# The four transposes of an expert's chunk: in one row ahead of the next chunk's up product, or one at a time between its steps

## What is computed

```python
def swiglu(t, wg, wu, wd):
    return (jax.nn.silu(t @ wg) * (t @ wu)) @ wd

def moe_ffn(h, router_w, wg, wu, wd):
    ...
    for e in range(N_EXPERTS):
        y = y + gates[:, e:e + 1] * swiglu(t, wg[e], wu[e], wd[e]).astype(jnp.float32)
```

## Time and profile before

| what | value |
|---|---|
| median of 3 runs | 1448.1 us (1447.97 to 1448.22) |
| the profiled execution | 1447.98 us |
| its span in the trace | 1446.2 us |
| PE busy | 1427.1 us (99%), 7084 matmuls |
| PE loads busy | 1189.5 us (82%) |
| DVE busy | 1194.8 us (83%) |
| ACT busy | 1034.2 us (72%) |
| granted TensorE clock, mean | 0.999 of 2.4 GHz |
| DMA | 454.11 MB, 314 GB/s over the span |

### The profile page before, as it was taken

One profiled execution on the slowest core, in us unless ns is written; L12 is line 12 of the kernel. 1 busy time (PEld: TensorE's weight loads), 2 busy tenths in 40 slices (PEclk: granted clock), 3 DMA queues, 4 the chain that ended last, 5 costly groups with the idle time before them and its releaser, 6 DMA issues.

```text
span 1446.2 us, 20820 instructions
## 1 busy us (share of the span) xinstructions
PE 1427.1 (99%) x7084; PEld 1189.5 (82%) x7084; DVE 1194.8 (83%) x1381; ACT 1034.2 (72%) x1280; POOL 18.6 (1%) x15
## 2 busy tenths in 40 slices
PE   9999999999999999999999999999999999999997
PEld 7988888887987788888888888888888888888885
DVE  7777565556877798899889999989889989889997
ACT  6766444455576677887787787787778778777775
POOL 0000000000000200000000000000000000001001
PEclk9999999999999999999999999999999999999999
DMA  9435965544524499999999999999999999999991
GB/s 374 176 130 210 372 236 204 201 174 175 183 110 160 164 422 402 355 403 382 364 394 389 380 368 398 381 363 392 384 351 397 390 378 370 393 375 373 420 394 71
DMA packets 68899, 454.11 MB, mean 314 GB/s; under 512 B 9456, under 2 KB 9712, under 8 KB 17008
## 3 DMA queue, kind: packets, MB, share of 16 engines
q1 hardware_dynamic: 61056, 432.47, 76.9%
q10 hardware_dynamic: 6640, 16.78, 3.3%
q0 software_dynamic: 1152, 4.19, 0.7%
HBM read 438.21 MB, written 15.20 MB: 314 GB/s over the span
## 4 chain that ended last, share of the span: by engine, by line
PE 94%; DVE 2%; ACT 2%; issue 1%; DMA 0%; DVEq 0%; SPq 0%; ACTq 0%
PE psum L493 26%; PE psum L495 26%; PE psum L494 26%; PE psum L845 7%; PE psum L848 3%; PE psum L907 2%; ACT lru_b L1025 1%; PE psum L500 1%; PE psum L664 0%; PE psum L605 0%; PE psum L520 0%; DVE xs L1442 0%; PE psum L890 0%; DMA gain<-gains 0%; ACT w_hi L1012 0%
## 5 line engine op out<-in xcount | busy, mean ns | idle before, releaser
L1330 DVE TENSOR_TENSOR w_lo<-ring,w_hi 128x1024 fp32r<-128x1024 f32 x812 | 941.0, 1219 | 51.9 <-ACT w_hi L1012 51.1
L1012 ACT ACTIVATE w_hi<-ring 128x1024 fp32r<-128x1024 f32 x812 | 807.4, 1053 | 55.2 <-PE psum L495 49.9
L493 PE MATMUL psum<-w_hi,hT_both 128*128 128x512 f32 (+1 forms) x1120 | 434.3, 388 | 1.3 <-DVE hT_both L1341 1.3
L495 PE MATMUL psum<-w_hi,hT_both 128*128 128x512 f32 (+1 forms) x1120 | 426.7, 381 | 0.0
L494 PE MATMUL psum<-w_lo,hT_both 128*128 128x512 f32 (+1 forms) x1120 | 425.9, 380 | 0.0
L493 PEld LDWEIGHTS psum<-w_hi,hT_both 128*128 128x128 f32 x1120 | 210.7, 188 | 42.7 <-DVE hT_both L1341 3.7
L495 PEld LDWEIGHTS psum<-w_hi,hT_both 128*128 128x128 f32 x1120 | 210.6, 188 | 41.2
L494 PEld LDWEIGHTS psum<-w_lo,hT_both 128*128 128x128 f32 x1120 | 211.0, 188 | 38.4 <-issue 0.4
L493 PE MATMUL psum<-w_hi,act_hi 128*128 128x512 f32 x560 | 218.7, 391 | 0.0
L495 PE MATMUL psum<-w_hi,act_lo 128*128 128x512 f32 x560 | 218.2, 390 | 0.0
L494 PE MATMUL psum<-w_lo,act_hi 128*128 128x512 f32 x560 | 218.2, 390 | 0.0
(11 more groups left out here) (243 smaller groups left out, 885.8 us busy)
## 6 DMA issues: line engine op xcount, KB each, us to landing
ring<-moe_gate SPq DMA_DIRECT2D x112, 1024.0 KB, 7.1
ring<-moe_up SPq DMA_DIRECT2D x112, 1024.0 KB, 7.5
ring<-moe_down SPq DMA_DIRECT2D x112, 1024.0 KB, 7.2
ring<-in_units SPq DMA_DIRECT2D x19, 1024.0 KB, 7.9
ring<-dense_gate SPq DMA_DIRECT2D x14, 1024.0 KB, 4.8
ring<-dense_up SPq DMA_DIRECT2D x14, 1024.0 KB, 4.8
ring<-dense_down SPq DMA_DIRECT2D x14, 1024.0 KB, 4.8
ring<-out_units SPq DMA_DIRECT2D x8, 1024.0 KB, 8.1
```

Of the source, the lines that this page charges most:

```text
L493: pe.matmul(dst, s_hi, m_hi, start=start, stop=False)
L495: return pe.matmul(dst, s_lo, m_hi, start=False, stop=stop)
L1012: act.activation(w_hi[:, h % AHEAD, :], ring[:, n % RING, (h % 2) * HCOLS:(h % 2 + 1) * HCOLS], ACT.Copy).then_inc(hi_ready, 1)
L1330: dve.tensor_tensor(w_lo[:, h % AHEAD, :], ring[:, (h // 2) % RING, (h % 2) * HCOLS:(h % 2 + 1) * HCOLS], w_hi[:, h % AHEAD, :].bitcast(F3 ...
```

## The change

On PE the function `turn_prod` is replaced by `turn_piece(c, f)`, which makes one of the four transposes: the wait for `prod_ready` is at the first piece, the increment of `prod_tr` at the last. For chunks 0 to 5 the pieces now stand inside the unit (up, c, 0) of the next chunk, one ahead of each of its four products. So three 512-column matmuls lie between one transpose and the next, where none did. The transposes of the seventh chunk stay in a row where they were. On ACT and DVE `turned_hi(c - 1)` and `turned_lo(c - 1)` move from ahead of the splits of (gate, c, 1) to ahead of the second split of (up, c, 0), that is behind three more splits. The number of instructions of each kind is the same.

```diff
             def expert_item(item, final):
-                def turn_prod(c):
-
-                    pe.wait_ge(prod_ready, item * ENC + (NCH + c + 1))
-                    for f in range(ETC):
-                        mm = pe.transpose(ps[6][:, f * C:(f + 1) * C], prod[:, c % 2, f * P:(f + 1) * P], ident)
-                    mm.then_inc(prod_tr, 1)
+                def turn_piece(c, f):
+
+                    if f == 0:
+                        pe.wait_ge(prod_ready, item * ENC + (NCH + c + 1))
+                    mm = pe.transpose(ps[6][:, f * C:(f + 1) * C], prod[:, c % 2, f * P:(f + 1) * P], ident)
+                    if f == ETC - 1:
+                        mm.then_inc(prod_tr, 1)
...
-                    if (kind, c, i) == ("up", c, 0) and c >= 1:
-                        turn_prod(c - 1)
...
-                        turn_prod(ENC - 1)
+                        for f in range(ETC):
+                            turn_piece(ENC - 1, f)
...
                             for k in range(2):
                                 kk = 4 * i + 2 * s + k
+                                if kind == "up" and i == 0 and c >= 1:
+                                    turn_piece(c - 1, 2 * s + k)
                                 mm = product(ps[2 * (c % 2) + (kind == "up")], hT(kk, 0, C), w(k),
...
-                    if kind == "gate" and i == 1 and c >= 1:
-                        turned_hi(c - 1)
...
                     for s in range(2):
                         h = 2 * (NPRE + n) + s + AHEAD
+                        if kind == "up" and i == 0 and s == 1 and c >= 1:
+                            turned_hi(c - 1)
                         if not final or h < 2 * (NPRE + NEU):
                             split_hi(h, item)
...
-                    if kind == "gate" and i == 1 and c >= 1:
-                        turned_lo(c - 1)
...
                     for s in range(2):
                         h = 2 * (NPRE + n) + s + AHEAD
+                        if kind == "up" and i == 0 and s == 1 and c >= 1:
+                            turned_lo(c - 1)
                         if not final or h < 2 * (NPRE + NEU):
                             split_lo(h, item)
```

## The result

The changed kernel takes 1454.7 us (median of 5 runs, 1454.56 to 1454.79) against 1448.1 us: **6.6 us more**, ratio 1.0046 with a 95% interval of 1.0035 to 1.0057. The forecast was 1451.4 us with a range up to 1453.6: the direction was right, the size (3.3 us) was half of what came, and the time lies outside the range.

The account below looks back on a forecast made before the run. PE's own stream was taken to bound the experts; the tail's +3.3 us, with the other terms at 0, on 1448.1 us gave 1451.4 us, range 1447.3 to 1453.6.

Parts of the forecast that it names:

- PE bounds the experts, and its own stream alone sets the end: Expert stage: PE is busy 200.00 of 200 us and never waits, so only its own stream moves the end.
- A lone transpose costs 0.109 us, nothing is hidden: PE, 192 moved transposes: each holds PE 0.109 us alone as in a row, so no gain, 192 x 0.
- the rival of the hidden load: PE: the load for the matmul behind a transpose is pulled ahead; 8.1 us less, 1440.0 us; chance 0.09.
- The 56 ns: Skill-page time for a 128-column matmul not held by its load; by it the transposes would save 10.2 us.
- The tail, +3.3 us: PE's large matmuls after an interruption run slower: 0.023 us for each of three new interruptions in 48 chunks, 3.3 us.
- the dense layer's 1.9: Low value for the tail, from the dense layer's alternating matmuls: 0.013 us a group, 1.9 us in all.
- DVE, 0 us: DVE's act_lo, three splits later, is ready at 32.2 and needed by PE's down at 33.3: 1.1 us left, cost 0.
- DVE comes too late: act_lo over 1.1 us later than placed, PE stands at down; 0.1 us in 48 chunks, +4.8 us, 1456.2; chance 0.07.
- The signs named beforehand: Changed trace: three large matmuls behind a transpose take 0.70 us, a chunk 16.87 us, PE not idle at down's first load.
- The sign against the forecast: An idle PE at down's first load, said beforehand to make the prediction wrong.

## Why the prediction was right in direction and wrong in size

- **PE bounds the experts, and its own stream alone sets the end:** right for the kernel before, where no load of PE in the experts waits. In the kernel after it no longer holds: 2.4 of the 6.6 us are PE's pace, the rest is PE standing for DVE.
- **A lone transpose costs 0.109 us, nothing is hidden:** right; 0.11 in the trace after, 0.109 + 0.03 to 0.05 for one alone. The load behind that of the transpose starts at 1014.00 with the transpose, and the next at 1014.11, so the rival of the hidden load is out. The Trainium skill, page "TensorE: Matmul & The Clock Gate", section "Architectural detail: the array is 16× 32×32, not 1× 128×128", says that loads can be pulled ahead of matmuls in flight and that a matmul can begin before its load is complete. The trace agrees with both, the first by one matmul and no more, the second in the row at 1014.03, but neither shortens the stream. The 56 ns from that page's section "Back-to-back issue gap" were not reached; the trace has 0.108 to 0.114 us.
- **The tail, +3.3 us:** the mechanism right, the size 2.4 us, between the dense layer's 1.9 and the 3.3 taken. I took 0.023 us for each new interruption; three cost 0.05 us, 0.016 each.
- **DVE, 0 us:** this is the step that failed, with some 4.2 to 4.3 of the 6.6 us. The placing by hand was good for the chunk for which it was made: 1.1 us to spare were forecast, and in that kind of chunk `act_lo` ends at 1001.19 + 0.69 = 1001.88 with down's load at 1002.89, 1.0 us. But it was done for one ordinary chunk and carried to all 48. The kernel before would have warned, as its two rows below this list show. At the first pair of an item `act_lo` ends at 979.05 + 0.68 = 979.73 and down's first load starts at 982.60, 2.87 us later, and from 966.90 on DVE has hardly any idle time (0.1 us) that three more splits could fill. In an ordinary chunk it is 3.75 us (1029.27 to 1033.02), and DVE also waits 1.20 us for ACT ahead of `act_lo`, which the splits can use. Three splits take 3 x 1.146 = 3.44 us: 0.57 more than the 2.87, as an estimate, close to the gap of 0.62. Behind `paired` the margin was 3.03 us (1368.95 to 1371.98), which makes 0.41 against the measured 0.43. So the failure could be worked out from the trace that the forecast used.
- **The rival "DVE comes too late"** named the place and the mechanism but got 0.07, with the even splits of one ordinary chunk as the reason against it. That its +4.8 us is near the measured 4.3 is luck: it is 0.1 us in each of 48 chunks, and what came is some 0.5 us in nine.
- **The signs named beforehand:** the three large matmuls behind a lone transpose take 0.70 us, as said, and a chunk 16.85 us instead of 16.87. The sign against the forecast, an idle PE at down's first load, is what came.

The rows of the kernel before at an item's first pair, from the timelines of DVE and of PE's loads:

```profile
979.05 0.68 DVE L1341 TENSOR_TENSOR act_lo<-psum,act_hi 128x512 fp32r<-128x512 f32 x1
```

```profile
982.60 0.19 PEld L493 LDWEIGHTS psum<-w_hi,act_hi 128*128 128x128 f32 x1
```

The two rows of the kernel after for the margin in an ordinary chunk, from the timeline of PE's loads and from that of DVE:

```profile
1002.89 0.19 PEld L493 LDWEIGHTS psum<-w_hi,act_hi 128*128 128x128 f32 x1
```

```profile
1001.19 0.68 DVE L1343 TENSOR_TENSOR act_lo<-psum,act_hi 128x512 fp32r<-128x512 f32 x1
```

## What to carry to other kernels

Where a step moves down an engine's hand-written list, find its reader and the time between the two in the **worst** turn of the loop: behind the boundary of the body, and in the copy of the body for the last turn with its extra work. An engine that has 10% to spare on average can still be late at one semaphore each turn. And these transposes of 128 columns hold PE for the same 0.11 us alone or in a row; scattering them between 512-column matmuls hid nothing here and paid for each interruption.

## What the runs showed of the hardware

After an interruption of a stream of 512-column float32r matmuls (0.2267 us each) by one to twelve transposes, the next five to ten take about 0.232 us each, then the old pace is back; this costs 0.03 to 0.05 us whatever the length. With one or four in a row two values 0.02 us apart come in turn (16.46 and 16.48, 16.79 and 16.81). What in the chip makes the tail was not tried and stays open.
